# Hybrid decoder layer on one core: other SBUF start addresses for TensorE's moving tensors

## What is computed

```python
a = rmsnorm(h, norm_mix_w)
u_s5, z_pool, q, k, v, g_lr, r = split(a @ w_in)     # 2048 -> 4112
mixed = concat([s5_mixer(u_s5), pool_mixer(z_pool), gla_mixer(q, k, v, g_lr, r)])
h = h + mixed @ w_out                                # 2048 -> 2048
up = rmsnorm(h, norm_ffn_w) @ w_up                   # 2048 -> 2 x 5632 (gate, value)
h = h + (silu(causal_conv3(gate)) * value) @ w_down  # 5632 -> 2048
gate = sigmoid(rmsnorm(h, norm_ple_w) @ w_pg)        # 2048 -> 2048
h = h + (p @ w_ple) * gate                           # 256 -> 2048
return rmsnorm(h, final_norm_w)
```

## Time and profile before

| | |
|---|---|
| median of 3 runs | 2210.57 us (2210.36 to 2210.83) |
| the profiled execution | a span of 2209.0 us; its own time beside the span is not given |
| TensorE (PE) busy | 2185.0 us, 99% of the span, 10892 matmuls |
| weight loads (PEld) busy | 1841.5 us, 83% |
| DVE, ScalarE, GpSimd busy | 1390.3, 886.1, 309.3 us |
| DMA | 322.05 MB, 146 GB/s |

### The profile page before, as it was taken

The page is one execution under the profiler, slowest core; times in us unless marked ns, Lnnn a source line. Parts: engine busy times, 40 slices in busy tenths (PEclk is TensorE's granted clock), DMA queues, the critical chain, the costliest instruction groups (busy, mean ns, idle before and its releaser), DMA issues.

```text
span 2209.0 us, 28981 instructions
## 1 busy us (share of the span) xinstructions
PE 2185.0 (99%) x10892; PEld 1841.5 (83%) x10892; DVE 1390.3 (63%) x1731; ACT 886.1 (40%) x1000; POOL 309.3 (14%) x332
## 2 busy tenths in 40 slices
PE   9999999999999999999999999999999999999997
PEld 7888878878888888888888888888888888888886
DVE  7486236553367988888888888886334333446444
ACT  6222245442242544454444454553222122226433
POOL 6993004000000111111111111110000000000001
PEclk9999999999999999999999999999999999999999
DMA  6423222133333777777777777766333332233222
GB/s 220 134 74 108 93 91 82 58 119 140 144 110 119 201 207 211 200 190 203 210 205 204 204 193 195 209 211 229 103 134 106 127 121 91 91 116 112 95 95 76
DMA packets 106037, 322.05 MB, mean 146 GB/s; under 512 B 8224, under 2 KB 56992, under 8 KB 85632
## 3 DMA queue, kind: packets, MB, share of 16 engines
q1 hardware_dynamic: 76112, 268.39, 33.7%
q0 software_dynamic: 29872, 52.96, 13.1%
HBM read 299.30 MB, written 22.02 MB: 145 GB/s over the span
## 4 chain that ended last, share of the span: by engine, by line
PE 87%; POOL 7%; DVE 2%; DMA 1%; ACT 1%; issue 1%; SPq 0%; DVEq 0%; POOLq 0%; ACTq 0%
PE bank L989 23%; PE bank L674 17%; PE bank L675 17%; PE bank L676 17%; PE bank L991 12%; PE bank L776 1%; DMA w_raw<-in_w_up 1%; DMA Y<-in_x 1%; DVE xs_lo L1541 1%; POOL QKV L2254 0%; POOL QKV L2274 0%; POOL Q L2295 0%; POOL Y L2290 0%; PE bank L852 0%; DVE x_block L1920 0%
## 5 line engine op out<-in xcount | busy, mean ns | idle before, releaser
L989 PE MATMUL bank<-x_block,w_hi 128*128 128x512 f32 x2240 | 777.8, 391 | 3.0 <-DVE w_lo L1926 1.6
L991 PE MATMUL bank<-x_block,w_lo 128*128 128x256 f32 x2240 | 629.4, 281 | 0.0
L1071 ACT ACTIVATE w_hi<-w_raw 128x2048 fp32r<-128x2048 f32 (+1 forms) x134 | 222.5, 1661 | 741.7 <-PE bank L676 733.8
L989 PEld LDWEIGHTS bank<-x_block,w_hi 128*128 128x128 f32 x2240 | 419.7, 187 | 94.6 <-DVE w_lo L1926 2.5
L674 PE MATMUL bank<-xs_hi,w_hi 128*128 128x512 f32 x1152 | 455.9, 396 | 4.7 <-DVE xs_lo L1543 2.8
L676 PE MATMUL bank<-xs_hi,w_lo 128*128 128x512 f32 x1152 | 449.0, 390 | 0.0
L675 PE MATMUL bank<-xs_lo,w_hi 128*128 128x512 f32 x1152 | 448.7, 390 | 0.0
L991 PEld LDWEIGHTS bank<-x_block,w_lo 128*128 128x128 f32 x2240 | 424.0, 189 | 0.0
L1519 DVE TENSOR_TENSOR w_lo<-w_raw,w_hi 128x2048 fp32r<-128x2048 f32 (+1 forms) x136 | 271.8, 1999 | 106.0 <-ACT w_hi L1071 103.3
L674 PEld LDWEIGHTS bank<-xs_hi,w_hi 128*128 128x128 f32 x1152 | 216.4, 188 | 55.0 <-issue 6.6
L675 PEld LDWEIGHTS bank<-xs_lo,w_hi 128*128 128x128 f32 x1152 | 216.4, 188 | 46.0 <-issue 2.6
(11 more groups left out here) (342 smaller groups left out, 2318.5 us busy)
## 6 DMA issues: line engine op xcount, KB each, us to landing
w_raw<-in_w_up SPq DMA_DIRECT2D x48, 1024.0 KB, 5.1
w_raw<-in_w_down SPq DMA_DIRECT2D x64, 704.0 KB, 4.1
Y<-in_w_up SPq DMA_DIRECT2D x40, 1024.0 KB, 6.6
w_raw<-in_w_in SPq DMA_DIRECT2D x31, 1024.0 KB, 4.8
Y<-in_w_up POOLq DMA_DIRECT2D x59, 512.0 KB, 6.7
Y<-in_w_up SPq DMA_DIRECT2D x39, 512.0 KB, 7.8
w_raw<-in_w_out SPq DMA_DIRECT2D x16, 1024.0 KB, 4.9
w_raw<-in_w_pg SPq DMA_DIRECT2D x16, 1024.0 KB, 4.7
```

Of the source, the lines that this page charges most:

```text
L989: nc.tensor.matmul(place(c, b, 0, 2), w_h[:, ks], xb[b][:, k, :, :].rearrange("p e t -> p (e t)"), start=fresh and k == 0, stop=False, ski ...
L991: last = nc.tensor.matmul(place(c, b), w_l[:, ks], xb[b][:, k, 0, :], start=False, stop=k == HALF_K - 1, skip_group_check=True)
L1071: nc.scalar.activation(w_hi[c % 2][:, 0:width], w_raw[c % 2][:, 0:width], ACT.Copy).then_inc(hi_made, 1)
```

## The change

Eleven lines of allocation. `params`, `norm4`, `iota_t` and a new unused tensor `edge` (96 bytes a partition) are allocated first, so xs and what lies over it starts 1920 bytes later. `powers` (640 bytes) moves between xs and the weights. `conv_in` is allocated after `val` and `u_two`. No instruction is changed; on every engine the same instructions stand in the same order with the same waits, so no order is shown here. The start addresses of the operands, in bytes of a partition, come out so:

| tensors | before | after |
|---|---|---|
| xs_hi, xs_lo | 16512, 49280: 128 modulo 2048 | 18432, 51200: 0 modulo 2048 |
| x_block3 to 6 (S1, A12, A22, S4) | 16512 + 16384 n: 128 modulo 2048 | 18432 + 16384 n: 0 modulo 2048 |
| mid_b_hi, mid_b_lo (second mid) | 16512, 39040: 128 modulo 2048 | 18432, 40960: 0 modulo 2048 |
| w_raw, w_hi, w_lo | from 82048: 128 modulo 2048 | from 84608: 640 modulo 2048, 128 modulo 512 |
| Y | 131200: 128 modulo 2048 | 133760: 640 modulo 2048, 128 modulo 512 |
| x_block0 to 2 (A11, S3, S2) | 201120, 168352, 184736: 416 modulo 2048 | 202368, 169600, 185984: 1664 modulo 2048, 128 modulo 512 |
| mid_a_hi, mid_a_lo (first mid) | 168352, 190880: 416 modulo 2048 | 169600, 192128: 1664 modulo 2048, 128 modulo 512 |
| p_lo, p_hi | 217504, 221600: 416 modulo 2048 | 218752, 222848: 128 modulo 512 |
| QKV, conv_acc, silu_g | 416 modulo 512 | 128 modulo 512 |
| val, u_two | 448 modulo 512 | 128 modulo 512 |

Each k-tile is 2048 bytes, so all k-tiles of a tensor share its remainder; a weight tile is 512 bytes.

```diff
--- before.py
+++ after.py
@@ -148,6 +148,11 @@
             return ctx.enter_context(nc.semaphore(name))
 
 
+        params = sb("params_sb", [P, N_PARAMS])
+        norm4 = sb("norm4", [P, 3, 4])
+        iota_t = sb("iota_sb", [P, BLOCKS])[:]
+        sb("edge", [P, 24])
+
         fast_x = ExitStack()
         xb = {b: sb(f"x_block{b}", [P, HALF_K, 2, HALF_T], F32R, fast_x) for b in (S1, A12, A22, S4)}
         fast_x.close()
@@ -157,6 +162,7 @@
         down_x.close()
         xs_hi = sb("xs_hi", [P, KT, SEQ], F32R)
         xs_lo = sb("xs_lo", [P, KT, SEQ], F32R)
+        powers = sb("powers", [P, 2, PAIRS, STEPS + 1])
         w_raw = [sb(f"w_raw{s}", [P, D]) for s in range(2)]
         w_hi = [sb(f"w_hi{s}", [P, D], F32R) for s in range(2)]
         w_lo = [sb(f"w_lo{s}", [P, D], F32R) for s in range(2)]
@@ -165,8 +171,6 @@
         rstd = sb("rstd", [P, SEQ])
         ones = sb("ones", [P, P])
         ident = sb("ident", [P, P])
-        norm4 = sb("norm4", [P, 3, 4])
-        params = sb("params_sb", [P, N_PARAMS])
 
         def par(name, i=0, n=1):
             if isinstance(i, int):
@@ -187,9 +191,7 @@
         intra = sb("intra", [P, PER_BATCH, P], where=s5)
         drive = [sb(f"drive{z}", [P, PER_BATCH, P], where=s5) for z in range(2)]
         y_blocks = sb("y_blocks", [P, PER_BATCH, BLOCKS], where=s5)
-        iota_t = sb("iota_sb", [P, BLOCKS], where=s5)[:]
         s5s = sb("s5s", [P, 20, PAIRS], where=s5)
-        powers = sb("powers", [P, 2, PAIRS, STEPS + 1], where=s5)
         back = sb("back", [P, 2, PAIRS, STEPS], where=s5)
         s5.close()
         gla = ExitStack()
@@ -233,9 +235,9 @@
         parts_p.close()
         conv_acc = sb("conv_acc", [P, SEQ])
         silu_g = sb("silu_g", [P, SEQ])
-        conv_in = sb("conv_in", [P, SEQ + 2])
         val = sb("val", [P, SEQ])
         u_two = sb("u_two", [P, 2, HALF_T])
+        conv_in = sb("conv_in", [P, SEQ + 2])
 
 
         p_raw = [conv_acc[:], silu_g[:]]
```

## The result

The changed kernel takes 2239.07 us (median of 4 runs, 2238.85 to 2239.29) against 2210.49: a ratio of 1.0128, 95% interval 1.0116 to 1.0140. The forecast was 2203.0; the change is slower by 28.6 us, and above the range. One execution of weights_at_zero, further down, took 3672.2 us at a granted clock of 0.555, where its three others had 0.997 or more, and is left out of that run's figures.

The account below looks back on a forecast made before the run. TensorE, busy 2185.0 of 2209.0 us, was taken as the bound. The terms -7.0 - 0.6 + 0 + 0 + 0 gave -7.6 us, from 2210.6 to 2203.0 us; range 2135 to 2215, about 0.83.

Parts of the forecast that it names:

- Steps (1) and (2): First mid tensor and p tensors, moved from 416 to 128 modulo 512: 6.6 ns less a matmul, -7.0 and -0.6 us.
- Step (4): xs, second mid tensor and four of seven blocks, moved from 128 to 0 modulo 2048: costed at 0.
- upper bound: Most that xs and second mid tensor could lose: 5.1 ns a matmul, from the gate's matmuls with 96 weight columns, 23.0 us.
- lower bound: Most that the 2048 starts could save: almost nothing over a matmul's columns, as in plain fp32, 77.8 us.
- nine matmuls: Plain fp32 matmuls of 512 columns moving Y, lasting 4.02 us: read as 428.5 ns each, 1.8 ns over two passes.
- Step (3): Blocks S3, S2 and A11 of the seven-product stage, moved from 416 to 128: 0 to 0.6 us, taken as 0.
- The second rival: xs and second mid matmuls: weights and moving tensor 128 bytes apart in phase, reads collide; 23.0 us slower, 2226; chance 0.15.
- P: Theory from the experiments: a matmul's price depends on the difference between the moving tensor's start and the weights'.
- L: Theory behind the forecast: only a start address that is no multiple of 64 bytes is dear.
- Step (5): Small tensors used only by DVE, ScalarE, GpSimd and DMAs change place: costed at 0, hidden by TensorE's work.

Follow-up runs that it names:

- weights_at_zero: Changed kernel with powers allocated behind ident instead of ahead of the weights, so the weights start at multiples of 2048: 2221.3 us, ratio to before 1.0052.
- first_mid_in_phase: Kernel before with 224 unused bytes right ahead of the first mid tensor, moving it and p to 128 modulo 256: 2202.99 us, ratio 0.9964.
- sweep_phase: Separate kernel without the layer: rows of 17 matmuls per pair of moving and weight start addresses; 226.7 ns settled where both are equal modulo 256.
- first_mid_alone: Kernel before with only first mid tensor, p and three blocks moved to 128 modulo 512: ten times, 2201.9 to 2202.7 or 2216.1 to 2217.3 us.

## Why the prediction was wrong

**Steps (1) and (2)**, the first mid tensor and p, were right in sign and size: 395 to 389 ns in the changed kernel, 7.8 us by first_mid_in_phase. The reason given for them was wrong, and that the number came out all the same is luck: the change happened to give these tensors the weights' own remainder. 416 was dear not as a number that is no multiple of 64 but because it is not the weights' remainder modulo 256.

**Step (4)** is the one that failed: "I take 0: 0 and 128 are both multiples of 64". Measured, 128 bytes between moving tensor and weights cost xs 5.4 ns a matmul (13.4 + 4.5 us, and the 0.6 that p gave back within them, 18.5 us over 3456) and the second mid tensor 6.6 to 7 ns, 7 us over 1056. Its upper bound, 23.0 us for the two from the gate's tile, was near the 25.5 measured, but by luck: 5.1 ns was read as a cost of the difference in place, and 96 weight columns cost (280.65 - 276.74) / 17 = 230.0 ns with both starts at 0 too (L109 and L110 of sweep_phase), so 3.4 of the 5.1 come with the narrower load. Its lower bound was an empty hope: no address that was tried gives less than 226.7 with 512 columns and a full load. It rested on plain fp32, whose "nine matmuls" are halves: the GLU's source has 16 matmuls where the page counts x32, so one of them takes two of those 428.5 ns. The four blocks, costed at 0 even in the upper bound, took a mean of 350.9 instead of 346.8 ns a pair over the stage, 5 us.

**Step (3)** failed too: the three blocks were to cost 0 to 0.6 us and cost 960 x 6.5 = 6 us (353.5 against 347.0 ns a pair, means over the stage), in phase and in the bad rhythm. The timeline of before showed no difference between 416 and 128, and I read that as no effect of the address on the pairs. It was one of several equal prices, held in place by the order of the blocks.

**The second rival** named the mechanism that came: weights and moving tensor 128 bytes apart. It got 0.15. What spoke against it was weak: the first mid tensor's 416 has a phase as well, I wrote, and took that as an objection, when it was the same effect seen from the other side. Before the change every cheap tensor shared the weights' remainder and the dear ones, the first mid tensor and p, did not, which fits P as well as L. Its price of 2226 left out the blocks, 11 us, and had 5.1 ns where about 5.7 came.

**Step (5)** held: DVE's, ScalarE's and GpSimd's busy times moved by less than 1 us.

## What to carry to other kernels

Where TensorE is the bound and works in the reduced fp32 form with 512 moving and 128 weight columns, allocate moving tensors and weights with the same remainder modulo 256 bytes; a pad of 224 bytes was worth 7.8 us here, and the change, which set xs, the second mid tensor and four blocks 128 bytes off, cost 28.6. For other shapes measure both. Where long and short matmuls alternate, the kernel that gained 7.8 us kept three of the seven blocks 32 bytes off and had one group of times; with all seven in phase there were two. Do not judge an address by itself: before concluding from two prices which property of an address matters, list the remainders of both operands, since every reading that they allow is a rival. And time a layout several times, for the same addresses can run in two rhythms.

## What the runs showed that I had not expected

- The price has memory. At a difference of 0, 96 matmuls in a row kept the rhythm that they settled into, and in the four profiles of first_mid_alone the stage did from 763 us to its end, 740 us or more; a delay of 0.15 us had exchanged it in one of them; five of the first ten executions of one program took 14.5 us more than the others.
- A moving tensor 4 bytes off costs 236.7 ns, with a load of 1 column as with 128; with 128 columns that is 10 ns over the price in phase.
- The reduced form pays 13.3 ns over 512 columns even in phase, where the 16-bit form pays 2.5. That it comes from reading four bytes a column at full rate is argued from the 16-bit and plain fp32 rows (215.8 ns, and 429.2 for each of the two matmuls that the profile shows for one of plain fp32, 2.5 over twice 213.3), not shown. What in the chip makes 256 the modulus stays open.
